# A decoder layer's sample attention: GpSimd's queue stores the decay rows first and asks for the last three sequences' cached values after the reload of the triangular systems

## The reference, cut to what matters

```
proj = (x * (1 + scale) + shift) @ w_in
mixer A: softmax attention in three groups, (window, dilation) = (128,1), (512,4), (2048,16);
         for samples the keys and values come from a cache of past positions and the new tokens
mixer B: gated DeltaNet, 6 heads of 128 x 128, in chunks:
    G     = cumsum(g)                                   # log decay inside a chunk
    dmask = exp(G_i - G_j) for i >= j
    lower = strict lower part of (kb @ k.T) * dmask
    sol   = solve(I + lower, [v * beta, kb * exp(G)])   # unit lower triangular system
    scan over chunks: v_new = u - w @ S; o = q*exp(G) @ S + intra @ v_new; S = S*exp(g_last) + k' @ v_new
out = (sigmoid(.) * branch_a + sigmoid(.) * branch_b) @ w_o;  x <- LayerNorm(alpha * x + gate * out)
```

## Time and profile before

| engine | busy us | share of the span |
|---|---|---|
| PE (products) | 2343.6 | 95% |
| DVE | 1587.7 | 65% |
| ACT | 1130.4 | 46% |
| POOL | 268.3 | 11% |

### The profile page before, as it was taken

How to read it: one execution, slowest core, us unless ns; L and a number is a source line. 1 busy time by engine, 2 the same in 40 slices (tenths; PEclk the granted TensorE clock), 3 DMA queues, 4 the chain that set the end, 5 groups by cost and what they waited for, 6 DMA issues and landing times. The chain is left out here.

```text
span 2454.4 us, 45084 instructions
## 1 busy us (share of the span) xinstructions
PE 2343.6 (95%) x16926; PEld 2069.5 (84%) x16926; DVE 1587.7 (65%) x4065; ACT 1130.4 (46%) x2381; POOL 268.3 (11%) x461
## 2 busy tenths in 40 slices
PE   5999999999999999999999999969998899999998
PEld 2777788888999999999999967648888699999886
DVE  6867676554453766767555377758996877665665
ACT  4444444444422444444444376737776533331323
POOL 0000000000121110110000000233321011111000
PEclk8999999999999999999999999989999699999999
DMA  7232323333432322233322290975565655556442
GB/s 263 95 112 95 112 101 106 105 118 108 170 101 82 101 99 92 102 117 98 112 94 98 77 370 36 338 243 153 162 189 195 203 156 181 172 159 219 141 142 99
DMA packets 231864, 350.78 MB, mean 143 GB/s; under 512 B 47830, under 2 KB 167230, under 8 KB 226400
## 3 DMA queue, kind: packets, MB, share of 16 engines
q1 hardware_dynamic: 175232, 217.09, 28.4%
q0 software_dynamic: 34400, 119.40, 12.7%
q10 hardware_dynamic: 22016, 11.40, 1.6%
HBM read 240.45 MB, written 107.39 MB: 142 GB/s over the span
## 5 line engine op out<-in xcount | busy, mean ns | idle before, releaser
L304 PE MATMUL ps_f<-m_lo,w_hi 128*128 128x272 f32 (+1 forms) x2436 | 790.0, 324 | 12.7 <-DVE m_lo L614 6.1
L304 PE MATMUL ps_f<-m_hi,w_hi 128*128 128x272 f32 (+1 forms) x2436 | 794.0, 326 | 0.0
L304 PE MATMUL ps_f<-m_hi,w_lo 128*128 128x272 f32 (+1 forms) x2436 | 785.2, 322 | 0.0
L304 PEld LDWEIGHTS ps_f<-m_lo,w_hi 128*128 128x128 f32 x2436 | 459.1, 188 | 67.6 <-issue 32.3
L304 PEld LDWEIGHTS ps_f<-m_hi,w_lo 128*128 128x128 f32 x2436 | 459.9, 189 | 37.0
L304 PEld LDWEIGHTS ps_f<-m_hi,w_hi 128*128 128x128 f32 x2436 | 459.0, 188 | 33.8
L678 DVE TENSOR_TENSOR stage<-partial,ps_f 128x512 f32<-128x512 f32 (+2 forms) x348 | 171.3, 506 | 318.8 <-PE ps_f L304 307.3
L429 ACT ACTIVATE partial<-ps_f 128x272 f32<-128x272 f32 (+1 forms) x348 | 160.8, 462 | 392.6 <-PE ps_f L304 390.9
L391 ACT ACTIVATE w_hi<-w_raw 128x512 fp32r<-128x512 f32 x348 | 213.1, 625 | 204.1 <-PE ps_f L304 128.1
L585 DVE TENSOR_TENSOR w_lo<-w_raw,w_hi 128x512 fp32r<-128x512 f32 x348 | 238.9, 687 | 85.1 <-ACT w_hi L391 81.5
L703 DVE SCALAR_TENSOR_TENSOR conv<-stage,side,conv 128x1024 f32<-128x1024 f32 x108 | 138.4, 1281 | 8.1 <-ACT conv L445 6.8
(11 more groups left out here) (531 smaller groups left out, 4433.2 us busy)
## 6 DMA issues: line engine op xcount, KB each, us to landing
w_raw<-in_w_feat SPq DMA_DIRECT2D x58, 1024.0 KB, 5.9
gates<-scratch_g_d SPq DMA_DIRECT2D x56, 256.0 KB, 3.1
z_f<-scratch_z_d ACTq DMA_DIRECT2D x13, 768.0 KB, 4.7
scratch_conv_d<-conv POOLq DMA_DIRECT2D x18, 544.0 KB, 3.0
scratch_conv_d<-conv POOLq DMA_DIRECT2D x18, 512.0 KB, 2.9
kc<-in_k_cache SPq DMA_DIRECT2D x8, 1152.0 KB, 15.0
vc<-in_v_cache POOLq DMA_DIRECT2D x8, 1152.0 KB, 16.9
w_ada<-in_w_ada SPq DMA_DIRECT2D x8, 1024.0 KB, 14.9
```

Source lines behind the costliest of these rows:

```text
L304: last = pe.matmul(out[:, 0:n], l[:, cols], r, start=start and k == 0 and nth == 0, stop=k == KH - 1 and nth == 2, skip_group_check=not start)
```

## The change

On POOL two things are moved, and nothing else changes. The store of the decay rows (with its wait for `row_put`) goes ahead of all loads of `vc`. The loads of sequences 5, 6 and 7 (with their wait for the prompt's last weighting) go behind the stores of the systems' blocks and behind POOL's half of the reload. All transfers, their sizes and the other engines' streams stay as they were.

```diff
             for c in range(2):
                 load_kq(pool, c, pair["xkq_first"][c])
+            pool.wait_ge(row_put, 1)
+            pool.dma_start(t["G_rows"].rearrange("b (h p) -> (b h) p", p=P), G_row[:, :]).then_inc(row_out, 16)
             pool.wait_ge(late["prompt_scored"], NG * NBLK)
             values(2, 3, 4)
             pool.wait_ge(late["stats_out"], 16 * 6)
             for g in range(NG):
                 pool.wait_ge(late["rows_out"][g], 16 * 4)
             values(0, 1)
-            pool.wait_ge(row_put, 1)
-            pool.dma_start(t["G_rows"].rearrange("b (h p) -> (b h) p", p=P), G_row[:, :]).then_inc(row_out, 16)
-            pool.wait_ge(late["prompt_weighed"], NG * NBLK)
-            values(5, 6, 7)
             for c in range(2):
                 pool.wait_ge(masked, 3 * c + 3)
                 for dst, src in system_blocks(t, c, UA[:, c], 1):
                     pool.dma_start(dst, src).then_inc(u_out[1], 16)
             for s in range(2):
                 pool.wait_ge(u_out[s], 64)
             pool.dma_start(pair["sub_u"][NSUB // 2:], system_of(t, 0)).then_inc(pair["sub_in"][1], 16)
+            pool.wait_ge(late["prompt_weighed"], NG * NBLK)
+            values(5, 6, 7)
             pool.wait_ge(pair["causal_in"], 32)
```

## The result

The changed kernel takes 2463.99 us, the median of 20 runs, where the kernel before took 2457.7 beside it (20 runs). The ratio is 1.0021 with a 95% interval of 1.0013 to 1.0029: about 5 us slower by the ratio, 6.3 between the medians. The forecast was 2454.4, counted from 2455.16, the three runs then known; the longer series beside the change has the kernel before at 2457.7, so 2.5 of the 9.6 us between forecast and result lie in that start. The profiled execution of the changed kernel took 2458.12 us (span 2456.3, mean clock 0.976), one of its lower times.

What follows compares the result with a forecast made beforehand. The prediction took the path through late block stores, POOL's reload and DVE's elimination as the bound. Of 9.3 us sooner, the smaller chain kept 8.8 - 8.0 = 0.8; 2456.28 - 0.8 - 1.12 = 2454.4 us, own range 2452 to 2456.5.

Steps and rivals of the forecast that it cites:

- Row store early, at no cost: POOL's decay-row store lands some 14 us sooner; ACT's earlier loads cost the first weighting 0 us, bounds 0 to 1.9.
- Blocks land by 1603.6, elimination 9.3 us sooner: Block stores, 2.0 us each, land at about 1603.6; after POOL's reload DVE starts at 1609.2 instead of 1618.47.
- Sequences 5 to 7 landed at 1622.0: Late loads on POOL's queue beside SP's 512-byte pieces take 13.4 us instead of 8.6; second weighting 6.4 us late.
- rival A: DMA queues alternate packet by packet: sequences land at 1617.9, L is 3.9, gain 4.9 us, time 2450.3; chance 0.27.
- 64%: Share POOL's queue was taken to keep beside SP's stream of small pieces while sequences 5 to 7 load, 0.264 MB/us.
- rival B: SP's loads and the last three sequences drain together, landing at 1625.0: L is 11.0 us, time say 2457.8; chance 0.20.
- Half clock in the second weighting, 1.6 us: PE idles about 7 us before the second weighting, so the clock dips and the weighting takes 1.6 us more.
- L: Lateness of all that follows PE's second weighting: 6.4 us for late sequences plus 1.6 for the clock, 8.0 us.
- Chain of the masks, gain 9.3 - L: PE's products of chunks 2 and 3, then the last mask, end at 1629.7 + L where it was 1639.0.
- Chain of SP's solution, gain 8.8 - L: Solution reload behind `att_s` and L2192's loads starts at 1631.0 + L, was 1635.95; with 3.9 us slack, gain 8.8 - L.
- I take what ACT's step at L2675 (1645.89) gains as what the kernel gains: From there DVE is 19.78 of 20 us busy and PE 18.20, so the step's 0.8 us gain was the kernel's.
- the third of the prediction's own signs of being wrong: The prediction is wrong if what ACT's step at L2675 gains is not what the kernel gains.

Runs made afterwards that it cites:

- e3: The changed kernel with SP's first solution store and reload ahead of the `att_s` store and the loads at L2203 and L2192: 2456.64 us, 0.9997 of the kernel before.
- e9: The changed kernel with only sequence 7 asked for behind the reload, 5 and 6 behind 0 and 1: 2461.54 us, 1.0007 of the kernel before.
- e4: The changed kernel with unread filler products on PE, seven ahead of the first weighting and five ahead of the second: 2468.08 us, 1.0042 of the kernel before.
- e7: The kernel of e3 with SP loading both reload halves and POOL asking for sequences 5 to 7 right behind its own block stores: 2458.01 us, 0.9998 of before.
- e13: The changed kernel with ACT, not SP, asking for the decay rows of chunks 4 and 5: 2464.83 us, 1.0019 of the kernel before.
- e8: The changed kernel, nothing edited, profiled a second time: the profiled execution took 2463.0 us.

## Why the prediction was wrong, step by step

- *Row store early, at no cost:* half right. It landed in 6.4 us. But ACT then asked for its 0.79 MB at 1594.53, and the first weighting started 23.4 to 23.7 us behind the copy instead of 21.4 to 21.7: 2.0 us, the upper bound given (1.9), where 0 was taken. In e1, with the row store alone, it was 22.7.
- *Blocks land by 1603.6, elimination 9.3 us sooner:* the last stores took 4.0 to 4.6 us, not 2.0, and POOL's reload went out at 1606.81. Taken from the copy, the elimination starts 7.9 us sooner (30.5 for 38.4), and a POOL addition stretches its first operation to 1.20 us.
- *Sequences 5 to 7 landed at 1622.0:* PE's first product that needs them starts at 1622.33, so the size is right (5.7 us late against 6.4), and its working is wrong, which is luck. The queues alternate one to one, 327 packets to 326, and in every single microsecond too (41 to 41, 43 to 42, 54 to 54, 47 to 46), and POOL's keeps 93.4% of the engines. That is the rule of rival A; 64% was wrong. From the first issue (1607.34) to that product it took 15.0 us, where the forecast has 17.1 and rival A 13.0; but the issue came 2.4 us later than the 1604.9 taken, 1.4 counted from the copy. The 208 to 41 packets behind the 64% were no fair contest: POOL's queue held only the end of one store there (L2276, issued at 1685.1, 6.0 us to landing). The prediction also set the Trainium skill ("DMA: Bandwidth & Descriptors", section "Queues, rings and completion order") beside rival B: a DMA engine drains a whole packet of some 9 to 17 descriptors from a queue at its turn. With as many descriptors a turn on both sides, that rule gives rival A's shares as well. If the profile's packets are its descriptors, the even counts in each microsecond speak against turns of that length.
- *Half clock in the second weighting, 1.6 us:* mis-sized. The window of the 72 products grew from 6.3 to 9.5 us, 3.2 more. So L, the lateness of what follows the second weighting, was 9.0 us (L2335 at 52.5 for 43.5) instead of 8.0.
- *Chain of the masks, gain 9.3 - L:* 0.3 by the measured L; the trace shows 0.5 (last mask at 57.8 for 58.3).
- *Chain of SP's solution, gain 8.8 - L:* -0.2 by the measured L; the solution landed in 4.9 us instead of 4.3, and the rest of ACT's 1.0 us (66.9 for 65.9) is in the same chain. Its slack of 3.9 us was right: the reload was 4.7 us late and ACT's step 1.0. With L past 8.8 the case named as rival B had come about, by another way: SP held the solution back behind `att_s`. e3 shows that this is the place, since undoing it takes the loss away.
- *"I take what ACT's step at L2675 (1645.89) gains as what the kernel gains":* the step that failed, and the third of the prediction's own signs of being wrong. ACT's step lost 1.1 us on the means, the kernel about 5; in e9, e4 and e7 it even gained 3 to 4 us on the kernel before, and none of them was faster. The step rested on 20 us from 1720 on, not on what comes right behind ACT's step: there DVE idled 7.86 us before `rv` and was 22.94 of 28 us busy, and its second elimination began right behind `rv`. The late solution also delays what SP issues behind it. First, the decay rows: POOL's additions move into DVE's second elimination and cost 1.8 to 2.0 us (27.5 and 27.3 us from `rv` on, for 25.5 and 25.8), shown by e13's profile, where they are gone, though e13's times are as high as the change's. Second, in some executions TensorE stays at half clock for some 27 us, 5.5 us more. One in three profiles of the change had it, and weighed so, 1.0 + 1.8 + 1.8 make the mean lateness of 4.6 us of these three. How the 5 us of the 20 runs divide is not shown: if the long stretch marks the upper times, most of the runs have it, and it is the larger part. What decides whether an execution has it stays open.

The rows that would have warned were in the trace of before: SP queues the next load of decay rows behind the solution's reload, the block stores of chunks 2 and 3 and its part of their reload, and POOL's additions ended 1.1 us ahead of the second elimination (1651.33 against 1652.44). And DVE idled behind ACT's step, for products of PE:

```profile
1650.37 0.87 DVE L2581 SCALAR_TENSOR_TENSOR rv<-ps_c,coef,bv 128x128 f32<-128x128 f32 x3 [7.86 <-PE ps_c L2428]
```

## What to carry to other kernels

Before a load is moved later, list what stands behind its consumer on every in-order queue: here one store of the finished attention held back the solution, the reload and the next decay rows, and putting the solution ahead of it was worth the whole loss. Lateness at one step is not the kernel's lateness: follow it until two profiles run about parallel again, here some 35 us further on, and look there for operations of VectorE and GpSimd that used to miss each other. Where a kernel's times fall into two groups, profile it more than once before explaining a few microseconds.

## What the runs showed of the hardware

- Two DMA queues with packets of 512 bytes and 8 KB shared the engines one packet each, 327 to 326 in 7 us, so the queue with small packets hardly slowed the other (93.4%).
- GpSimd's addition of 128x768 stretched a VectorE operation with two inputs from 0.18 to 1.80 us.
- TensorE stayed at the lower clock level for 27.3 us while it was 24.25 us busy (e8), where the same place in two other executions of the same program had 6.8 and 10.2 us of it. In the change's first profile the clock went down after a stretch with little PE work, 1.98 us busy in 6.2, and came back after 6.8 us:

```profile
1640.00:1646.20 6.20, 1.98 (x17) 1.53 (x15) 0.36 (x1) 4.66 (x18) 4.34 (x8) 1.00 0.38 82
1646.20:1653.00 6.80, 5.97 (x77) 5.51 (x78) 2.65 (x9) 3.32 (x12) 0.64 (x2) 0.50 0.72 156
```

The rows give PE, weight loads, DVE, ACT and POOL busy, clock, DMA share and GB/s.
